# Latent attention: q and k without their rotated part made channels-first, rotated parts turned four heads at a time, scores of two heads side by side

## The chip, the cores and the metric

One core of a Trainium2 chip runs the whole program; the other cores are idle. The metric is the device time of one execution in microseconds, the median of three runs. The program is one fp32 forward pass through two models behind one another, and all matrix weights are streamed from HBM once.

## The reference

`x` is 256 tokens x 1024 channels. A first block has a state-space layer and an attention layer; a second block has two layers (`DEPTH2`), each with three branches (latent attention, convolution, retention) that are gated and merged, and a feed-forward part. The change touches only the latent attention of these two layers:

```python
q = (rms_norm_2(c_q, q_norm) @ w_uq).reshape(B, S, 8, 64 + 32)      # c_q: 256 channels
q_nope, q_pe = q[..., :64], apply_rope(q[..., 64:], cos, sin)
kv = (rms_norm_2(c_kv, kv_norm) @ w_ukv).reshape(B, S, 8, 64 + 64)  # c_kv: 128 channels
k_nope, v = kv[..., :64], kv[..., 64:]
k_pe = apply_rope(k_pe, cos, sin)                                   # one, shared by all heads
s = einsum('bqhd,bkhd->bhqk', q_nope, k_nope) + einsum('bqhr,bkr->bhqk', q_pe, k_pe)
p = softmax(s * 96 ** -0.5)                                         # no mask: 256 x 256
o = einsum('bhqk,bkhd->bqhd', p, v)
```

## The kernel before

**Weights.** A list of slots (up to two k-tiles of 128 x 512 weights each) is streamed by SP into six or eight buffers. Each slot is split: ScalarE copies it to fp32r as `weights_hi` (`make_hi`, L1249), VectorE takes the rest, `weights_lo` (`make_lo`, L1780), and TensorE makes each product from three fp32r matmuls, hi x hi, hi x lo and lo x hi. `tile_slot` (L705 to L707) has 128 tokens as the stationary operand and streams the weights (512 columns wide, 384 for `uq`), so its result has tokens on the partitions; `hidden_slot` (L683 to L685) has 128 weight columns as the stationary operand and streams 256 tokens, so its result has channels on the partitions. `run(n)` does the next n slots of the list. ScalarE and VectorE walk the same list in program order, up to `AHEAD` = 4 slots ahead of TensorE, and empty the accumulators (`evac`) where a chunk of slots ends. The four accumulator banks `acc` are used by parity of the chunk: chunk n waits for the reader of chunk n - 2 (`reader_of`).

**Latent attention of a layer.** `lat_norm_T` is turned (L800) and split into `mla_F_hi` and `mla_F_lo`. Two slots `uq` (two k-tiles, 384 columns: four heads of 96) and two slots `ukv` (one k-tile, 512 columns) make `mla_q_T`, `mla_k_T` and `mla_v_T` with tokens on the partitions. VectorE rotates 32 of each head's 96 channels (`mla_rope`) and writes the shared rotated k into all eight heads. Then `heads` goes over eight heads, one at a time: TensorE turns q and k of the head (four transposes to 96 x 128, L1004), ScalarE copies them to `m_qk_F` (L1612), TensorE makes the scores with a contraction over 96 rows (two matmuls of 256 columns, L1020), VectorE finds the maximum, ScalarE takes the exponential and divides (L1630, L1606), TensorE turns the probabilities (four transposes, L1013), ScalarE copies them, and for every second head `mla_product` multiplies two heads at once: each has 64 value channels, and the two write to partitions 0 to 63 and 64 to 127 of one bank, two column halves of the array (L1071).

**What fills the time between these steps.** Each step is followed by `mla_gap`, which runs two slots of ordinary weight work (retention and gate projections, 36 slots of a layer), so that the other engines have time. The order on each engine is written out by hand; waits are on semaphores. VectorE also has the 31 taps of the convolution (`taps`) spread over the gaps.

A plain fp32 matmul leaves two MATMUL records in the trace, a transpose or an fp32r matmul one.

## Time and profile before

| | |
|---|---|
| median of three runs | 1236.92 us (1236.46 to 1237.2) |
| the profiled execution | 1240.36 us |
| its span | 1238.5 us |
| TensorE busy | 1207.6 us, 98% |
| VectorE busy | 902.3 us, 73% |
| ScalarE busy | 638.7 us, 52% |
| granted TensorE clock | 0.998 of 2.4 GHz |

The span is what the profiler saw between the first and last instruction; the profiled execution took 1.9 us more than that and 3.4 us more than the median of the runs. In the timeline a row is a run of like instructions: start, time, engine, line, operation, tiles and count. TensorE is pipelined, so a record's length (0.39 us for 512 columns) is not what it costs; the distance of the starts is.

### The profile page before, as it was taken

Reading aid. Unit: us, or ns where it says so; the run is one execution under the profiler, and the core shown is the slowest. Engines: PE = TensorE matmul, PEld = TensorE weight load, DVE = VectorE, ACT = ScalarE, POOL = GpSimd, SP = SyncE. Lnnn points to the kernel's source line nnn. Section 1 sums busy time; section 2 is a strip of 40 time slices with the busy share of each in tenths; the row PEclk is TensorE's granted clock in tenths of the full one; section 3 lists DMA queues with packets and bytes.
Section 4 is the critical chain, followed back from the end, with each engine's and each line's share of the span. In section 5 each row is a group of like instructions: output and inputs, shape, how many; then the busy total and the mean of one; then the engine's idle time right before and its main releaser. Section 6 shows DMA issues by size and latency. Waiting matters only on the chain.

```text
span 1238.5 us, 19034 instructions
## 1 busy us (share of the span) xinstructions
PE 1207.6 (98%) x7597; PEld 1015.8 (82%) x7597; DVE 902.3 (73%) x1463; ACT 638.7 (52%) x1034; POOL 102.3 (8%) x163
## 2 busy tenths in 40 slices
PE   7999999999999999999999999999999999999998
PEld 3566778887978888787999987988788787999986
DVE  7998867767598998687656555589998687665553
ACT  4334565575547665546434443556575535444441
POOL 6400011101000200201000001000200201000000
PEclk9999999999999999999999999999999999999999
DMA  7735566444565455355666664565445355556552
GB/s 253 210 103 178 200 210 191 152 130 154 162 202 166 151 160 188 124 179 170 208 187 187 187 190 155 174 217 171 154 153 180 139 174 170 188 195 196 191 194 75
DMA packets 71958, 215.68 MB, mean 174 GB/s; under 512 B 16256, under 2 KB 19744, under 8 KB 71744
## 3 DMA queue, kind: packets, MB, share of 16 engines
q1 hardware_dynamic: 65008, 206.37, 52.0%
q0 software_dynamic: 2112, 6.97, 1.9%
q10 hardware_dynamic: 4752, 1.14, 0.4%
q8 instruction: 60, 0.98, 0.3%
q14 instruction: 26, 0.21, 0.1%
HBM read 208.95 MB, written 3.15 MB: 171 GB/s over the span
## 4 chain that ended last, share of the span: by engine, by line
PE 82%; DVE 10%; ACT 5%; issue 2%; POOL 1%; DMA 0%; SPq 0%; DVEq 0%; POOLq 0%; ACTq 0%
PE acc L705 16%; PE acc L706 16%; PE acc L707 16%; PE acc L683 7%; PE acc L684 7%; PE acc L685 7%; PE acc L642 3%; DVE weights_lo L1780 2%; PE mixed L1020 1%; ACT junk L1284 1%; PE mixed L1117 1%; PE turned L760 1%; ACT weights_hi L1249 1%; DVE h_T L1810 1%; PE mixed L1004 1%
## 5 line engine op out<-in xcount | busy, mean ns | idle before, releaser
L1780 DVE TENSOR_TENSOR weights_lo<-weights_raw,weights_hi 128x1024 fp32r<-128x1024 f32 (+1 forms) x304 | 356.1, 1206 | 67.2 <-ACT weights_hi L1249 66.3
L1249 ACT ACTIVATE weights_hi<-weights_raw 128x1024 fp32r<-128x1024 f32 (+1 forms) x304 | 305.6, 1043 | 77.2 <-DMA weights_raw<-stream_dram 77.0
L705 PE MATMUL acc<-weights_hi,act_F_hi 128*128 128x512 f32 (+1 forms) x656 | 264.8, 404 | 4.2 <-DVE weights_lo L1780 2.5
L707 PE MATMUL acc<-weights_hi,act_F_lo 128*128 128x512 f32 (+1 forms) x656 | 256.7, 391 | 0.0
L706 PE MATMUL acc<-weights_lo,act_F_hi 128*128 128x512 f32 (+1 forms) x656 | 256.5, 391 | 0.0
L683 PE MATMUL acc<-act_F_hi,weights_hi 128*128 128x256 f32 x624 | 175.1, 281 | 0.0
L684 PE MATMUL acc<-act_F_hi,weights_lo 128*128 128x256 f32 x624 | 173.9, 279 | 0.0
L685 PE MATMUL acc<-act_F_lo,weights_hi 128*128 128x256 f32 x624 | 173.9, 279 | 0.0
L705 PEld LDWEIGHTS acc<-weights_hi,act_F_hi 128*128 128x128 f32 x656 | 123.6, 188 | 32.6 <-DVE weights_lo L1780 3.6
L707 PEld LDWEIGHTS acc<-weights_hi,act_F_lo 128*128 128x128 f32 x656 | 123.4, 188 | 26.8
L706 PEld LDWEIGHTS acc<-weights_lo,act_F_hi 128*128 128x128 f32 x656 | 123.7, 189 | 24.0
L685 PEld LDWEIGHTS acc<-act_F_lo,weights_hi 128*128 128x128 f32 x624 | 118.3, 190 | 0.0
L683 PEld LDWEIGHTS acc<-act_F_hi,weights_hi 128*128 128x128 f32 x624 | 117.3, 188 | 0.2
L684 PEld LDWEIGHTS acc<-act_F_hi,weights_lo 128*128 128x128 f32 x624 | 117.3, 188 | 0.2
L1810 DVE SCALAR_TENSOR_TENSOR conv_acc_F<-conv_in_F,conv_params,conv_acc_F 128x256 f32<-128x256 f32 x240 | 98.0, 480 | 0.0
L1780 DVE TENSOR_TENSOR weights_lo_more<-weights_raw_more,weights_hi_more 128x1024 fp32r<-128x1024 f32 (+1 forms) x60 | 71.5, 1215 | 18.0 <-ACT weights_hi_more L1249 17.8
L1810 DVE SCALAR_TENSOR_TENSOR ffn_tanh_F<-ffn_tanh_F,acc 128x512 f32<-128x512 f32 (+1 forms) x24 | 15.4, 642 | 93.4 <-ACT ffn_tanh_F L1369 88.8
L1249 ACT ACTIVATE weights_hi_more<-weights_raw_more 128x1024 fp32r<-128x1024 f32 (+1 forms) x60 | 61.6, 1048 | 26.0 <-DMA weights_raw_more<-stream_dram 25.8
L1369 ACT ACTIVATE ffn_tanh_F<-acc 128x512 f32<-128x512 f32 x20 | 12.0, 598 | 119.1 <-PE acc L685 119.1
L642 PE MATMUL acc<-weights_raw,hn_F 128*128 128x512 f32 x128 | 59.1, 609 | 1.2 <-DMA weights_raw<-stream_dram 1.2
L683 PE MATMUL acc<-act_F_hi,weights_hi_more 128*128 128x256 f32 x208 | 58.2, 280 | 0.0
L684 PE MATMUL acc<-act_F_hi,weights_lo_more 128*128 128x256 f32 x208 | 57.9, 279 | 0.0
(351 smaller groups left out, 1969.6 us busy)
## 6 DMA issues: line engine op xcount, KB each, us to landing
weights_raw<-stream_dram SPq DMA_DIRECT2D x306, 512.0 KB, 3.6
weights_raw_more<-stream_dram SPq DMA_DIRECT2D x58, 512.0 KB, 3.6
gains<-rows_dram POOLq DMA_DIRECT2D x12, 512.0 KB, 4.7
weights_raw<-stream_dram SPq DMA_DIRECT2D x6, 416.0 KB, 3.1
weights_raw<-stream_dram SPq DMA_DIRECT2D x4, 384.0 KB, 3.9
x_T<-x_in_dram SPq DMA_DIRECT2D x4, 256.0 KB, 6.4
ssm_bc<-ssm_bc_dram SPq DMA_DIRECT2D x1, 1024.0 KB, 8.1
u_scratch<-u_T ACTq DMA_DIRECT2D x4, 256.0 KB, 6.2
```

Of the source, the lines that this page charges most:

```text
L642: i = pe.matmul(acc[par][t][:, 0:w], f0[:, k, t * P:(t + 1) * P], whole(pos, slice(kk * w, (kk + 1) * w)), start=first and kk == 0, stop=l ...
L683: pe.matmul(o, wh, hi[:, k, :], start=first and kk == 0 and m % 2 == 0, stop=False, skip_group_check=True)
L684: pe.matmul(o, wl, hi[:, k, :], start=False, stop=False, skip_group_check=True)
L685: i = pe.matmul(o, wh, lo[:, k, :], start=False, stop=last and kk == s["nk"] - 1, skip_group_check=True)
L705: pe.matmul(o, xh, wh, start=first and kk == 0, stop=False)
L706: pe.matmul(o, xh, wl, start=False, stop=False)
L707: i = pe.matmul(o, xl, wh, start=False, stop=last and kk == s["nk"] - 1)
L760: i = pe.transpose(turned_bank[n % 2][:, kk * P:(kk + 1) * P], src(t, 4 * half + kk), ident)
L1004: x = pe.transpose(b[0:dk, (2 * n + t) * P:(2 * n + t + 1) * P], src(t, i), ident)
L1249: act.activation(high(s, slice(0, n)), whole(s, slice(0, n)), ACT.Copy).then_inc(hi_made, 1)
L1780: dve.tensor_tensor(low(s, slice(0, n)), whole(s, slice(0, n)), high(s, slice(0, n)).bitcast(F32), ALU.subtract).then_inc(lo_made, 1)
L1810: return dve.scalar_tensor_tensor(out=o, in0=a, scalar=s, in1=b, op0=op0, op1=op1)
```

## The change

Four things change in both layers. (1) The 64 unrotated channels of q and k of two heads are made with channels on the partitions (`latent_slot`, `qn` and `kn`: head 2p on partitions 0 to 63, head 2p + 1 on 64 to 127); the rotated parts of q of all eight heads come with the second `uq` slot, with tokens on the partitions; v as before. The split of a `uq` slot goes to two tiles in three pieces. (2) The rotated q is turned for four heads at once and the rotated k once, written four times over (`turned_rope`: six transposes a layer instead of 32). (3) The scores of two heads are made together: first contraction over 64 rows, head 2p in rows 0 to 63 of the array and head 2p + 1 in rows 64 to 127, into two banks; then the rotated part, contraction over 32 rows, added into the same banks (`mla_scores`). (4) The order goes by pairs: probabilities of two heads are turned together, and into the banks `turned`. `mla_gap` stands 18 times with work in it, as before.

```diff
-                mq = sb("mla_q_T", [P, TT, MLA_H, MQK], F32, s5)
-                mk = sb("mla_k_T", [P, TT, MLA_H, MQK], F32, s5)
-                mv = sb("mla_v_T", [P, TT, MLA_H, MV], F32, s5)
...
+                sb("latent_lows", [P, 1024], F32, s5)
+                qn = sb("mla_q_nope_F", [P, MLA_H // 2, SEQ], F32, s5)
+                mq = sb("mla_q_rope_T", [P, TT, MLA_H, ROPE], F32, s5)
+                mk = sb("mla_k_rope_T", [P, TT, 4, ROPE], F32, s5)
+                qr = sb("mla_q_rope_F", [P, 2, SEQ], F32, s5)
+                kr = sb("mla_k_rope_F", [P, SEQ], F32, s5)
+                kn = sb("mla_k_nope_F", [P, MLA_H // 2, SEQ], F32, s5)
+                mv = sb("mla_v_T", [P, TT, MLA_H, MV], F32, s5)
...
-                "uq.": (mla_q_copied, 4 * l + n), "ukv.": (mla_v_copied, 4 * l + n),
+                "uq.": (mla_copied, 7 * l + (n - 1 if i else 1)), "ukv.": (mla_copied, 7 * l + 3 + n),
...
+            def latent_slot(s, par):
+                _, kind, half = split_name(s["chunk"])
+                q = kind == "uq."
+                k0 = 0 if q else QR // P
+                pe.wait_ge(lo_made, pos + 1 - WHOLE)
+                for t in range(TT):
+                    who, value = reader_of(acc_user[par], t)
+                    pe.wait_ge(who, value)
+                for kk in range(s["nk"]):
+                    for m in range(2):
+                        cols = slice(m * P, (m + 1) * P)
+                        wh = high(pos, slice(kk * SEQ + m * P, kk * SEQ + (m + 1) * P))
+                        wl = uq_lo[:, half, kk, cols] if q else ukv_lo[:, half, cols]
+                        o = acc[par][0][:, m * SEQ:(m + 1) * SEQ]
+                        pe.matmul(o, wh, c_hi[:, k0 + kk, :], start=kk == 0 and m == 0, stop=False, skip_group_check=True)
+                        pe.matmul(o, wl, c_hi[:, k0 + kk, :], start=False, stop=False, skip_group_check=True)
+                        i = pe.matmul(o, wh, c_lo[:, k0 + kk, :], start=False, stop=kk == s["nk"] - 1, skip_group_check=True)
+                if q and not half:
+                    return i
+                for t in range(TT):
+                    for kk in range(s["nk"]):
+                        xh, xl = (f[:, k0 + kk, t * P:(t + 1) * P] for f in (c_hi, c_lo))
+                        if q:
+                            wh, wl = uqr_hi[:, kk, :], uqr_lo[:, kk, :]
+                        else:
+                            wh, wl = high(pos, slice(4 * NOPE, 4 * (NOPE + MV))), ukv_lo[:, half, 4 * NOPE:]
+                        o = acc[par][1][:, t * SEQ:(t + 1) * SEQ]
+                        pe.matmul(o, xh, wh, start=t == 0 and kk == 0, stop=False, skip_group_check=True)
+                        pe.matmul(o, xh, wl, start=False, stop=False, skip_group_check=True)
+                        i = pe.matmul(o, xl, wh, start=False, stop=kk == s["nk"] - 1, skip_group_check=True)
...
+                def turned_rope():
+                    pe.wait_ge(mla_roped, 2 * TT * (l + 1))
+                    b = mix(f"L{l}.mla.qr", qk_copied, HEADS + 2 * l + 1)
+                    for n in range(2):
+                        for t in range(TT):
+                            x = pe.transpose(b[:, n * SEQ + t * P:n * SEQ + (t + 1) * P],
+                                             mq[:, t, 4 * n:4 * n + 4, :].rearrange("p h d -> p (h d)"), ident)
+                    x.then_inc(mixed, 1)
+                    b = mix(f"L{l}.mla.kr", qk_copied, HEADS + 2 * l + 2)
+                    for t in range(TT):
+                        x = pe.transpose(b[:, t * P:(t + 1) * P], mk[:, t, :, :].rearrange("p h d -> p (h d)"), ident)
+                    x.then_inc(mixed, 1)
+                def mla_scores(pair):
+                    pe.wait_ge(mla_copied, 7 * l + 6)
+                    pe.wait_ge(qk_copied, HEADS + 2 * (l + 1))
+                    heads_of = [2 * pair + e for e in range(2)]
+                    b = [mix(f"L{l}.mla.s{h}", probs_made, 2 * (HEADS + MLA_H * l + h + 1)) for h in heads_of]
+                    for qt in range(TT):
+                        for e in range(2):
+                            rows_ = slice(NOPE * e, NOPE * (e + 1))
+                            pe.matmul(b[e][:, qt * SEQ:(qt + 1) * SEQ], qn[rows_, pair, qt * P:(qt + 1) * P], kn[rows_, pair, :],
+                                      start=(qt == 0), stop=False, skip_group_check=True)
+                    for qt in range(TT):
+                        for e in range(2):
+                            a = NOPE * e + ROPE * (pair % 2)
+                            x = pe.matmul(b[e][:, qt * SEQ:(qt + 1) * SEQ], qr[a:a + ROPE, pair // 2, qt * P:(qt + 1) * P],
+                                          kr[a:a + ROPE, :], start=False, stop=(qt == TT - 1), skip_group_check=True)
+                            if qt == TT - 1:
+                                x.then_inc(mixed, 1)
+                def turned_probs(pair):
+                    pe.wait_ge(probs_scaled, 2 * (HEADS + MLA_H * l + 2 * pair + 2))
+                    wait_turned(len(turn_at))
+                    for e in range(2):
+                        probs_at[f"L{l}.{2 * pair + e}"] = pos
+                        for qt in range(TT):
+                            for kt in range(TT):
+                                n = 2 * kt + qt
+                                x = pe.transpose(turned_bank[e][:, n * P:(n + 1) * P], m_p[:, e, qt, kt * P:(kt + 1) * P], ident)
+                        x.then_inc(mla_probs_turned, 1)
...
-                heads(f"L{l}.mla", MLA_H, MQK, lambda t, h: mq[:, t, h, :], lambda t, h: mk[:, t, h, :], m_qk, m_p, m_pt,
-                      HEADS + MLA_H * l, False, lambda h: (mla_roped, 2 * TT * (l + 1)), mla_gap, mla_product,
-                      [lambda: turned_ret_qk(0), lambda: turned_ret_qk(1)])
+                turned_rope()
+                mla_gap()
+                for i in range(MLA_H // 2 + 1):
+                    if i > 0:
+                        turned_probs(i - 1)
+                    if i < MLA_H // 2:
+                        mla_scores(i)
+                    else:
+                        turned_ret_qk(0)
+                    mla_gap()
+                    mla_gap()
+                    if i == MLA_H // 2:
+                        turned_ret_qk(1)
+                    if i > 0:
+                        mla_product(i - 1)
+                    mla_gap()
+                    mla_gap()
                 for h in range(2, RH):
...
-                act.activation(high(s, slice(0, n)), whole(s, slice(0, n)), ACT.Copy).then_inc(hi_made, 1)
+                if ".uq." in slots[s]["chunk"]:
+                    for o, x in uq_high(s):
+                        i = act.activation(o, x, ACT.Copy)
+                    i.then_inc(hi_made, 1)
+                elif ".ukv." in slots[s]["chunk"]:
+                    act.activation(by_part(high(s, slice(0, n))), by_head(whole(s, slice(0, n))), ACT.Copy).then_inc(hi_made, 1)
+                else:
...
                         act.activation(conv_t[:, t, :], b, ACT.Tanh, scale=0.5).then_inc(read, 1)
-                    elif kind == "uq.":
-                        act.activation(mq[:, t, 4 * i:4 * i + 4, :], b.rearrange("p (h d) -> p h d", h=4), ACT.Copy).then_inc(read, 1)
+                    elif kind in ("uq.", "ukv.") and t == 0:
+                        act.activation((qn if kind == "uq." else kn)[:, 2 * i:2 * i + 2, :].rearrange("p h q -> p (h q)"),
+                                       acc[table[name]["par"]][0][:, :], ACT.Copy).then_inc(read, 1)
+                    elif kind == "uq." and i == 1:
+                        act.activation(mq[:, :, :, :].rearrange("p t h d -> p (t h d)"), acc[table[name]["par"]][1][:, :],
+                                       ACT.Copy).then_inc(read, 1)
                     elif kind == "ukv.":
-                        v = b.rearrange("p (h d) -> p h d", h=4)
-                        act.activation(mk[:, t, 4 * i:4 * i + 4, 0:NOPE], v[:, :, 0:NOPE], ACT.Copy)
-                        act.activation(mv[:, t, 4 * i:4 * i + 4, :], v[:, :, NOPE:NOPE + MV], ACT.Copy).then_inc(read, 1)
+                        act.activation(mv[:, :, 4 * i:4 * i + 4, :],
+                                       acc[table[name]["par"]][1][:, :].rearrange("p (t h d) -> p t h d", t=TT, h=4),
+                                       ACT.Copy).then_inc(read, 1)
                     elif kind == "ret." and i < 4:
                         act.activation(rv[:, t, odd], b, ACT.Copy).then_inc(read, 1)
                     elif kind == "ret.":
```

TensorE in the first of the two layers, one step of the heads before. Names: `mla_q_T` and `mla_k_T` are q and k with tokens on the partitions, `m_qk_F` both turned; rows with 512 columns are slots, three a k-tile and tile of tokens.

```order
L1071 MATMUL turned<-m_probs_T,mla_v_T 64x256 x4
L1004 MATMUL mixed<-consts,mla_q_T 96x128 x2
L1004 MATMUL mixed<-consts,mla_k_T 96x128 x2
L705 MATMUL acc<-weights_hi,act_F_hi 128x512
...
L1013 MATMUL mixed<-consts,m_probs 128x128 x4
L1020 MATMUL mixed<-m_qk_F 128x256 x2
L705 MATMUL acc<-weights_hi,act_F_hi 128x512
```

The same place with the change, a step of a pair of heads:

```order
L1176 MATMUL turned<-consts,m_probs 128x128 x8
L1157 MATMUL mixed<-mla_k_nope_F,mla_q_nope_F 128x256 x4
L1162 MATMUL mixed<-mla_k_rope_F,mla_q_rope_F 128x256 x4
L772 MATMUL acc<-weights_hi,act_F_hi 128x512
...
L1188 MATMUL turned<-m_probs_T,mla_v_T 64x256 x4
L772 MATMUL acc<-weights_hi,act_F_hi 128x512
```

The four transposes ahead of every head are gone; the two score matmuls of a head are now eight of a pair, half over 64 and half over 32 rows; the product stands between slots instead of ahead of transposes. Ahead of the first pair the new transposes stand once:

```order
L1139 MATMUL mixed<-consts,mla_q_rope_T 128x128 x4
L1144 MATMUL mixed<-consts,mla_k_rope_T 128x128 x2
```

ScalarE where the four latent slots are emptied, before (names: `conv_tanh` is the reader of the chunk ahead of them):

```order
L1343 ACTIVATE conv_tanh<-acc 128x512 x2
L1249 ACTIVATE weights_hi<-weights_raw 128x1024
L1345 ACTIVATE mla_q_T<-acc 128x384 x2
L1249 ACTIVATE weights_hi<-weights_raw 128x1024
L1345 ACTIVATE mla_q_T<-acc 128x384 x2
L1348 ACTIVATE mla_k_T<-acc 128x4x64
L1349 ACTIVATE mla_v_T<-acc 128x256
```

and with the change:

```order
L1479 ACTIVATE conv_tanh<-acc 128x512 x2
L1385 ACTIVATE weights_hi<-weights_raw 128x1024
L1481 ACTIVATE mla_q_nope_F<-acc 128x512
L1385 ACTIVATE weights_hi<-weights_raw 128x1024
L1481 ACTIVATE mla_q_nope_F<-acc 128x512
L1484 ACTIVATE mla_q_rope_T<-acc 128x512
L1481 ACTIVATE mla_k_nope_F<-acc 128x512
L1487 ACTIVATE mla_v_T<-acc 128x2x256
```

Twelve copies of a layer are now seven wider ones, at the same place among the splits of the weights.

## Rows read from the trace of the kernel before

**Rows 1.** The page: busy time by engine, and the chain by engine.

```profile
PE 1207.6 (98%) x7597; PEld 1015.8 (82%) x7597; DVE 902.3 (73%) x1463; ACT 638.7 (52%) x1034; POOL 102.3 (8%) x163
PE 82%; DVE 10%; ACT 5%; issue 2%; POOL 1%; DMA 0%; SPq 0%; DVEq 0%; POOLq 0%; ACTq 0%
```

**Rows 2.** Busy time by window: the heads of both layers (length, then engines).

```profile
361.80:482.00 120.20, 120.20 (x579) 97.27 (x578) 111.86 (x213) 74.23 (x141) 6.70 (x1) 1.00 0.52 163
833.00:953.00 120.00, 120.00 (x576) 97.07 (x575) 111.52 (x213) 74.81 (x143) 6.69 (x1) 1.00 0.50 163
```

**Rows 3.** Timeline of TensorE: transposes of the first head among slots.

```profile
361.76 0.39 PE L707 MATMUL acc<-weights_hi,act_F_lo 128*128 128x512 f32 x1
361.99 0.38 PE L1004 MATMUL mixed<-consts,mla_q_T 128*96 128x128 f32 x2
...
362.66 0.40 PE L706 MATMUL acc<-weights_lo,act_F_hi 128*128 128x512 f32 x1
```

**Rows 4.** Timeline of TensorE: scores of the first head among slots.

```profile
367.70 0.40 PE L707 MATMUL acc<-weights_hi,act_F_lo 128*128 128x512 f32 x1
367.94 1.03 PE L1020 MATMUL mixed<-m_qk_F 96*128 96x256 f32 x4
...
369.03 0.39 PE L706 MATMUL acc<-weights_lo,act_F_hi 128*128 128x512 f32 x1
```

**Rows 5.** Timeline of TensorE: product of two heads, columns split in halves.

```profile
399.68 0.40 PE L707 MATMUL acc<-weights_hi,act_F_lo 128*128 128x512 f32 x1
400.00 1.08 PE L1071 MATMUL turned<-m_probs_T,mla_v_T 128*64 128x256 f32 x8
401.02 0.42 PE L1004 MATMUL mixed<-consts,mla_q_T 128*96 128x128 f32 x2
...
401.73 0.40 PE L706 MATMUL acc<-weights_lo,act_F_hi 128*128 128x512 f32 x1
```

**Rows 6.** Timeline of TensorE: eight tiles of 64 rows x 32 columns, two row halves.

```profile
99.07 2.03 PE L913 MATMUL turned<-c_mats_alt,states 64*32 64x128 f32 x128
101.03 2.41 PE L642 MATMUL acc<-weights_raw,hn_F 128*128 128x512 f32 x5
```

**Rows 7.** Groups of instructions by form: weight loads of 128 and of 64 columns.

```profile
L1020 PEld LDWEIGHTS mixed<-m_qk_F 96*128 96x128 f32 x64 | 11.0, 190 | 1.0
L1071 PEld LDWEIGHTS turned<-m_probs_T,mla_v_T 128*64 128x64 f32 x64 | 3.9, 136 | 3.6 <-issue 2.5
```

**Rows 8.** Timeline of TensorE: the latent slots of the first layer.

```profile
332.37 0.33 PE L705 MATMUL acc<-weights_hi,mla_F_hi 128*128 128x384 f32 x1
...
336.54 0.39 PE L705 MATMUL acc<-weights_hi,mla_F_hi 128*128 128x512 f32 x1
...
339.28 0.39 PE L705 MATMUL acc<-weights_hi,act_F_hi 128*128 128x512 f32 x1
```

**Rows 9.** Timeline of ScalarE at the same place.

```profile
332.58 1.08 ACT L1343 ACTIVATE conv_tanh<-acc 128x512 f32<-128x512 f32 x2 [0.24 <-PE acc L685]
336.19 1.06 ACT L1249 ACTIVATE weights_hi<-weights_raw 128x1024 fp32r<-128x1024 f32 x1 [0.66 <-DMA weights_raw<-stream_dram]
337.15 0.85 ACT L1345 ACTIVATE mla_q_T<-acc 128x384 f32<-128x384 f32 x2
```

**Rows 10.** Timelines of VectorE and TensorE: after the rotation, first layer.

```profile
344.11 5.76 DVE L1780 TENSOR_TENSOR weights_lo<-weights_raw,weights_hi 128x1024 fp32r<-128x1024 f32 x5
344.54 0.40 PE L707 MATMUL acc<-weights_hi,act_F_lo 128*128 128x512 f32 x1
345.38 0.50 PE L705 MATMUL acc<-weights_hi,act_F_hi 128*128 128x512 f32 x1 [0.44 <-DVE weights_lo L1780]
```

**Rows 11.** Timelines of ScalarE and TensorE: the latent slots of the second layer.

```profile
807.82 0.85 ACT L1345 ACTIVATE mla_q_T<-acc 128x384 f32<-128x384 f32 x2
...
802.66 0.28 PE L684 MATMUL acc<-act_F_hi,weights_lo 128*128 128x256 f32 x1
...
803.23 0.33 PE L705 MATMUL acc<-weights_hi,mla_F_hi 128*128 128x384 f32 x1
```

189 lines of the change are left out of this document (138 added, 51 removed).

## The prediction

> **What bounds the kernel now.** I read the page first: TensorE is busy 98% of the span and is 82% of the chain that ended last [rows 1]. Then busy time by window, for the two stretches in which the heads run: TensorE has no gap in either, VectorE is busy 111.9 of 120.2 us and ScalarE 74.2 us [rows 2]. So in these stretches time is what TensorE's own instructions take, and work taken from ScalarE or VectorE (12 copies of a layer become seven, eight copies of `m_qk_F` become two) gives nothing by itself. The change has to pay on TensorE, or in a wait of TensorE. I therefore read TensorE's timeline for the distance of starts. The slots give the rule: 12 matmuls of 512 columns from 336.54 to 339.28 are 0.228 us each, 24 of 384 columns from 332.37 are 0.174 us each [rows 8], and five starts of 256 columns from 802.66 to 803.23 are 0.114 us each [rows 11].
>
> **Transposes, the gain.** From the last slot matmul ahead of a head's four transposes to the second one behind them there are 0.90 us [rows 3]; two slot matmuls are 0.46 us of it, so four transposes cost 0.44 us, 0.11 us each. The change takes out 32 a layer and puts in six: 52 fewer in two layers, **5.7 us** less. Nothing covers them before, and nothing else would have run in that time, since TensorE waits for nobody there.
>
> **Scores, streaming: nothing.** Two score matmuls of a head (four records) cost 369.03 - 367.70 - 0.46 = 0.87 us [rows 4], 0.218 us a record, so a pair of heads 1.74 us. The pair now issues eight matmuls, 16 records, of the same 256 columns: one behind another 3.49 us, two at a time 1.74 us. Does the chip do two at a time? Two heads' product does it with column halves: eight records, which would be 1.74 us in a row, took 1.02 us [rows 5]. With row halves I have one place, 128 records of 128 columns in eight tiles, 64 rows x 32 columns, in 1.96 us [rows 6]. By the row of the scores a record of 128 columns is 0.109 us, so four column tiles alone would need 128 x 0.109 / 4 = 3.5 us: the two row halves ran side by side, and into two banks, as here. I take 1.74 us a pair, no change.
>
> **Scores, changing the shape of the array.** Around the product the trace shows a cost that isn't streaming: from the slot matmul at 399.68 to that at 401.73 are 2.05 us, of which 0.46 are slots, 0.44 the transposes and 0.87 the eight records two at a time; 0.28 us remain, for going to halves and back [rows 5], 0.14 us each way. The product keeps its two. The scores ran on the whole array and had none; now each pair goes from the whole to 64 rows, to 32 rows and back, three changes, 24 in two layers: 24 x 0.14 = **3.4 us** more. From 64 to 32 rows the trace shows nothing. The lower end is nothing at all (from transposes to slots the rows show no such cost [rows 3]); the upper is 0.19 us, since the first weights behind a change are 128 columns here and 64 in the product, and the load record is 190 against 136 ns [rows 7]. I take 0.14 for all 24, because the product is the nearest row. The Trainium skill (TensorEngine Tiling (Array Packing), Key Properties) says that a change of tiling mode drains the engine, and lists 64 and 32 rows as different modes. By it all 24 count; were the step from 64 to 32 rows free, 16 would, 1.1 us less.
>
> **Latent slots.** `uq` is 36 matmuls of 256 columns instead of 24 of 384: 4.10 against 4.17 us; `ukv` 24 of 256 instead of 12 of 512: 2.74 against 2.74 [rows 8, 11]. In two layers **0.1 us** less.
>
> **A wait at the second `ukv` slot.** `latent_slot` waits for both readers of its banks before its first matmul; for the second `ukv` slot these are the two copies behind the second `uq` slot, now 512 columns each, 1.08 us for two such copies [rows 9]. ScalarE comes to them after a split that waited for its DMA until 336.19 and took 1.06 us, so they end at 338.3. TensorE would be there at 332.37 + 48 x 0.114 = 337.8: it waits 0.5 us. Behind it stand all slots, but a cover follows: TensorE stands from 344.77 (344.54 + 0.23) to 345.38 for `weights_lo`, which VectorE makes late because of the rotation [rows 10]. Arriving 0.5 us later it waits 0.1 instead of 0.6, and VectorE, whose k part now writes four heads and not eight, isn't later. First layer: -0.1 us (not counting the cover: +0.5). Second layer: TensorE at 803.23 + 5.47 = 808.7, the copies start at 807.82 + 0.08 at the earliest and end at 809.0: 0.3 us, and no stall follows that would cover it. Together **0.2 us** more; between 0 and 0.8.
>
> **Costed at nothing.** The splits of the two `uq` slots are three pieces on ScalarE and VectorE instead of one; they are made some slots ahead, while VectorE waits. Copies, maxima, exponentials and divisions of the heads are as many as before but come in twos: between a pair's scores and the turning of its probabilities lie eight slots, 22 us, and between turning and product four, 11 us, against some 10 us and 2 us of work. If that cover were gone, each late copy (0.6 us) would be TensorE's. VectorE has 8 us to spare in a stretch of 120 and the same work in it. DMA issues and their order are the same, and SP's waits hang on slots that end within half a us of where they did.
>
> **Sum.** -5.7 + 0 + 3.4 - 0.1 + 0.2 = -2.2 us. It is made on one profiled execution (1240.4 us, span 1238.5), which lies 3.4 us above the median of the runs; no term of it is a share, so I take it off the median: 1236.9 - 2.2 = **1234.7 us**. With a change of shape at 0 it is 1231.3 us; with 0.19 us and the wait at its upper end, 0.8, it is 1236.5: the forecast's own range.
>
> **Rivals.**
>
> *Weight loads are not hidden behind matmuls in row tiles* (slower). Two matmuls at a time have four loads of 128 columns for every two steps; 64 columns more cost 54 ns of load [rows 7], so 128 cost 0.108 us. If the next load for a row half waits until the running matmul of that half is done, each step of 0.218 us becomes 0.326: eight steps a pair, eight pairs, 6.9 us, and 1241.6 us. Against it: slots of 256 columns come every 0.114 us though each has such a load in the same rows, and the eight small tiles kept pace [rows 6], with loads of 32 columns only. It decides as soon as more than a third of each load is exposed. The Trainium skill (TensorE: Matmul & The Clock Gate, The mechanism) says that a load overlaps running matmuls only where the row groups differ. Taken at its word it gives this case; the slots speak against it.
>
> *The halves don't run side by side.* The change then doesn't do what it says: 1.74 us a pair more, 13.9 us, 1248.6 us. Only [rows 6] speaks against it for row halves, and no row has row halves with all 128 columns.
>
> *Waits in twos.* VectorE is 93% busy in the heads [rows 2]. It now does two maxima in a row (each with a wait) before the next splits. If one split of 1.2 us came late once a layer, and the first layer's cover failed, 1.2 x 2 + 0.5 less what the forecast gains: 1237.6 us. TensorE's place four slots behind is against it.
>
> *Changes of shape cost nothing where both sides are ready*: 1231.3 us. The 0.28 us at the product speak against it.
>
> **Chances.** Forecast 0.66, loads exposed 0.10, one behind another 0.04, waits in twos 0.14, free changes 0.06. A difference under 0.2%, 2.5 us, is about what a measurement of this kernel can't tell from none; the forecast sits close to that line, so its 0.66 splits into 0.36 below 1234.4 and 0.30 above. Faster: 0.36 + 0.06 = 0.42. Same: 0.30 + 0.12 = 0.42. Slower: 0.02 + 0.10 + 0.04 = 0.16. The range 1231.3 to 1239.5 leaves out the two slow rivals and a little on either side.
>
> **What would show it.** In the changed profile: 12 transposes of rotated parts and no others for q and k; a pair's eight unrotated records in about 0.9 us and the eight rotated ones in about 0.9 us, with starts two by two; from slot to slot around them 1.74 + 0.4 us. Exposed loads would show as 1.3 us for eight records, no concurrency as 1.74. At the second `ukv` slot a wait of TensorE for ScalarE of 0.3 to 0.5 us, and the stall for `weights_lo` after the first layer's rotation nearly gone. Wrong I would be through any idle time of TensorE inside the heads, or a pair's scores over 2.5 us.

## The result and the profile after

| | us |
|---|---|
| before, median of 4 runs beside the changed kernel | 1237.06 (1236.46 to 1237.70) |
| changed kernel, median of 4 runs | 1261.01 (1260.88 to 1261.99) |
| ratio, 95% interval | 1.0195 [1.0182, 1.0208] |
| profiled execution of the changed kernel: its time, its span | 1260.88, 1259.1 |

The change costs 24 us. The prediction was 1234.7 us with a range to 1239.5, and all but 0.16 of the chance on "faster" and "same": it was wrong. In the lines from here on, a row of waits is: who waited for whom, us in total, times, longest. The page of the changed kernel: busy time, the chain that ended last by engine and by line, and two of the costliest groups.

```profile
PE 1212.1 (96%) x7657; PEld 1012.5 (80%) x7657; DVE 901.5 (72%) x1471; ACT 627.9 (50%) x1020; POOL 96.0 (8%) x163
...
PE 60%; DVE 25%; ACT 9%; issue 3%; POOL 1%; DMA 1%; SPq 0%; DVEq 0%; POOLq 0%; ACTq 0%
PE acc L772 10%; PE acc L774 10%; PE acc L773 10%; DVE weights_lo L1971 8%; PE acc L713 7%; PE acc L714 7%; PE acc L715 7%; DVE conv_acc_F L2001 7%; PE acc L676 3%; ACT weights_hi L1385 2%; PE mixed L1246 1%; ACT m_probs L1845 1%; ACT m_probs L1851 1%; DMA weights_raw<-stream_dram 1%; ACT junk L1420 1%
...
L1971 DVE TENSOR_TENSOR weights_lo<-weights_raw,weights_hi 128x1024 fp32r<-128x1024 f32 x296 | 348.6, 1215 | 98.1 <-ACT weights_hi L1385 97.2
...
L772 PE MATMUL acc<-weights_hi,act_F_hi 128*128 128x512 f32 (+1 forms) x656 | 264.6, 403 | 21.4 <-DVE weights_lo L1971 19.7
```

Against [rows 1] VectorE's busy time is the same within 1 us, but its share of the chain went from 10 to 25% and TensorE's from 82 to 60. Work did not grow; an engine with the same work became the one that others wait for. The last two rows say which wait: over the whole span VectorE's splits (`weights_lo`) stand 97.2 us behind ScalarE's halves (`weights_hi`), 66.3 before, and TensorE's slots 19.7 us behind VectorE's, 2.5 before. The same two head windows as in [rows 2], then TensorE's waits over the whole span, changed and before:

```profile
361.80:482.00 120.20, 111.06 (x520) 85.90 (x519) 96.31 (x184) 63.00 (x125) 4.79 (x1) 0.99 0.47 145
833.00:953.00 120.00, 113.05 (x525) 87.92 (x524) 97.11 (x184) 58.14 (x116) 4.75 (x1) 0.97 0.47 149
```

```profile
PE acc L772 <- DVE weights_lo L1971: 19.7, 14, 3.5
PE acc L705 <- DVE weights_lo L1780: 2.5, 5, 0.7
```

TensorE, gapless before, now idles 9.1 and 7.0 us in the windows, and all three engines do less in the same time. VectorE and ScalarE waiting for each other shows in the waits of 361 to 490 us. The last row is the second one in the kernel before:

```profile
ACT m_probs L1845 <- DVE m_stat L2007: 34.2, 4, 13.0
DVE weights_lo L1971 <- ACT weights_hi L1385: 24.8, 9, 3.2
ACT m_probs L1851 <- DVE m_stat L2722: 16.2, 4, 4.9
DVE weights_lo L1780 <- ACT weights_hi L1249: 7.5, 7, 1.8
```

The first pair of heads, step by step: VectorE's timeline, then ScalarE's (start, length).

```profile
373.62 0.17 DVE L2007 TENSOR_SCALAR m_stat<-m_stat 128x2 f32<-128x2 f32 x1
376.98 2.36 DVE L1971 TENSOR_TENSOR weights_lo<-weights_raw,weights_hi 128x1024 fp32r<-128x1024 f32 x2 [3.19 <-ACT weights_hi L1385]
379.26 3.25 DVE L2001 SCALAR_TENSOR_TENSOR conv_acc_F<-conv_in_F,conv_params,conv_acc_F 128x256 f32<-128x256 f32 x8
382.43 0.22 DVE L2722 RECIPROCAL m_stat<-m_stat 128x2 f32<-128x2 f32 x2
385.30 2.36 DVE L1971 TENSOR_TENSOR weights_lo<-weights_raw,weights_hi 128x1024 fp32r<-128x1024 f32 x2 [2.66 <-ACT weights_hi L1385]
```

```profile
373.09 0.47 ACT L1845 ACTIVATE m_probs<-mixed,m_stat 128x256 f32<-128x256 f32 x1 [6.61 <-DVE m_stat L2007]
...
375.89 2.00 ACT L1385 ACTIVATE weights_hi<-weights_raw 128x1024 fp32r<-128x1024 f32 x2
377.79 1.08 ACT L1491 ACTIVATE h_T<-acc 128x512 f32<-128x512 f32 x2
382.61 1.71 ACT L1851 ACTIVATE m_probs<-m_probs,m_stat 128x256 f32<-128x256 f32 x4 [3.75 <-DVE m_stat L2722]
```

VectorE ends the pair's two maxima at 373.8 and goes straight to its splits. Their halves come only behind ScalarE's four exponentials and four decays, from 375.89: VectorE stands 3.19 us. It then makes eight taps (3.25 us) before the reciprocals, and ScalarE stands 3.75 us for those, with its next halves queued behind the divisions; so VectorE stands another 2.66 us. That is 5.85 us in each of four steps, 23.4 us a layer, on an engine that I had credited with 8 to spare.

Where the 24 us lie: from the transposes of `h` ahead of the heads to those of `conv_acc_F` behind them the first layer takes 202.6 us instead of 191.6, the second 203.1 instead of 190.6: 23.4 us more. TensorE's own instructions take 1.3 us less than before (measured below, on a kernel with the same TensorE instructions and without these waits), so 24.7 us have to be found. Of these TensorE is idle 9.1 and 8.5 us (128.20 - 119.06 and 129.40 - 120.89, windows from 370 and 848 us to the stretch's end), in ten waits. From start to start such a wait costs some 0.25 us more than its idle time (the record ahead of it lasts 0.39 us where the next one would have started after 0.23): 2.5 us. The rest is the clock. After the longest wait, 3.5 us, and after two in the second layer the granted clock falls:

```profile
440.00:448.00 8.00, 6.80 (x23) 5.44 (x24) 5.59 (x12) 4.25 (x8) 0.00 (x0) 0.79 0.12 31
894.00:902.00 8.00, 7.09 (x24) 5.69 (x25) 8.00 (x14) 5.55 (x8) 0.00 (x0) 0.79 0.34 116
918.00:926.00 8.00, 5.64 (x18) 4.57 (x19) 5.66 (x12) 4.25 (x9) 0.00 (x0) 0.79 0.20 66
```

0.79 of 8 us is 3.4 us at the lower level, 1.2 GHz. Compared start by start with the kernel that has the same TensorE instructions and no such waits, the three stretches put TensorE 4.5 us behind; the heads of before have none. 17.6, 2.5 and 4.5 us are 24.6.

TensorE's steps themselves went nearly as forecast, the scores of the first pair:

```profile
367.50 0.40 PE L774 MATMUL acc<-weights_hi,act_F_lo 128*128 128x512 f32 x1
367.83 1.13 PE L1157 MATMUL mixed<-mla_k_nope_F,mla_q_nope_F 64*128 64x256 f32 x8
368.90 1.13 PE L1162 MATMUL mixed<-mla_k_rope_F,mla_q_rope_F 32*128 32x256 f32 x8
369.96 0.51 PE L772 MATMUL acc<-weights_hi,act_F_hi 128*128 128x512 f32 x1
370.30 0.40 PE L773 MATMUL acc<-weights_lo,act_F_hi 128*128 128x512 f32 x1
```

Measured as the prediction measured them, from the last slot matmul ahead to the second behind less two slots, the sixteen records take 370.30 - 367.50 - 0.46 = 2.34 us, where the forecast had 2.16 and two heads before took 1.74. The halves do run side by side and their loads are hidden; three changes of shape cost 0.60 us instead of 0.42. Of that 0.10 us lie ahead of the first record, 0.11 in the slot matmul behind, which takes 0.34 us instead of 0.23, and 0.20 in each of the two phases of eight records, 1.07 us instead of 0.87.

### The profile page after: what moved, and what is told of

The parts are those of the page before. It is cut to its first block, busy times and chain, and to the rows that moved or that the text cites. A ratio compares the mean times of both kernels' runs of the same rounds, so it can differ in the third digit from the quotient of the medians.

```text
span 1259.1 us, 19130 instructions
## 1 busy us (share of the span) xinstructions
PE 1212.1 (96%) x7657; PEld 1012.5 (80%) x7657; DVE 901.5 (72%) x1471; ACT 627.9 (50%) x1020; POOL 96.0 (8%) x163
## 4 chain that ended last, share of the span: by engine, by line
PE 60%; DVE 25%; ACT 9%; issue 3%; POOL 1%; DMA 1%; SPq 0%; DVEq 0%; POOLq 0%; ACTq 0%
PE acc L772 10%; PE acc L774 10%; PE acc L773 10%; DVE weights_lo L1971 8%; PE acc L713 7%; PE acc L714 7%; PE acc L715 7%; DVE conv_acc_F L2001 7%; PE acc L676 3%; ACT weights_hi L1385 2%; PE mixed L1246 1%; ACT m_probs L1845 1%; ACT m_probs L1851 1%; DMA weights_raw<-stream_dram 1%; ACT junk L1420 1%
## 5 line engine op out<-in xcount | busy, mean ns | idle before, releaser
L1971 DVE TENSOR_TENSOR weights_lo<-weights_raw,weights_hi 128x1024 fp32r<-128x1024 f32 x296 | 348.6, 1215 | 98.1 <-ACT weights_hi L1385 97.2
L1385 ACT ACTIVATE weights_hi<-weights_raw 128x1024 fp32r<-128x1024 f32 x296 | 298.3, 1050 | 71.9 <-DMA weights_raw<-stream_dram 71.7
L772 PE MATMUL acc<-weights_hi,act_F_hi 128*128 128x512 f32 (+1 forms) x656 | 264.6, 403 | 21.4 <-DVE weights_lo L1971 19.7
L774 PE MATMUL acc<-weights_hi,act_F_lo 128*128 128x512 f32 (+1 forms) x656 | 259.3, 395 | 0.0
L774 PEld LDWEIGHTS acc<-weights_hi,act_F_lo 128*128 128x128 f32 x656 | 124.6, 190 | 26.6
L2001 DVE SCALAR_TENSOR_TENSOR conv_acc_F<-conv_in_F,conv_params,conv_acc_F 128x256 f32<-128x256 f32 x240 | 106.5, 512 | 0.0
L715 PE MATMUL acc<-act_F_lo,weights_hi_more 128*128 128x256 f32 x208 | 57.5, 276 | 0.0
```

The source lines that it names most:

```text
L715: i = pe.matmul(o, wh, lo[:, k, :], start=False, stop=last and kk == s["nk"] - 1, skip_group_check=True)
L772: pe.matmul(o, xh, wh, start=first and kk == 0, stop=False)
L774: i = pe.matmul(o, xl, wh, start=False, stop=last and kk == s["nk"] - 1)
L1385: act.activation(high(s, slice(0, n)), whole(s, slice(0, n)), ACT.Copy).then_inc(hi_made, 1)
L1971: dve.tensor_tensor(low(s, slice(0, n)), whole(s, slice(0, n)), high(s, slice(0, n)).bitcast(F32), ALU.subtract).then_inc(lo_made, 1)
L2001: return dve.scalar_tensor_tensor(out=o, in0=a, scalar=s, in1=b, op0=op0, op1=op1)
```

## The experiments

Theory A: the order of work on VectorE and ScalarE makes them wait for each other, and VectorE has no room for it. Rival B: TensorE's own new work. Rival C: the granted clock by itself. Rival D: that heads come in pairs, whatever the order. Times are medians, ratios to the kernel before in the same call.

**The order undone, one engine at a time.** Four kernels from the changed one. On VectorE, the taps first:

```diff
+                    n = tapped[0]
+                    tapped[0] = min(n + 1, 2 * MLA_H + 2)
+                    taps(...)
                     run(min(2, fillers[0]))
                     splits(pos + AHEAD)
...
-                    n = tapped[0]
-                    tapped[0] = min(n + 1, 2 * MLA_H + 2)
-                    taps(...)
```

> Edit: in each gap VectorE does its share of the convolution's taps first and its share of the splits behind them, so the halves that ScalarE makes after the exponentials are looked at 3 us later. Theory A (VectorE and ScalarE wait for each other within a step of two heads; 24.8 us of VectorE's idle time in the first layer's heads stand in front of weights_lo): the wait of VectorE for weights_hi behind two maxima shrinks from 3.2 us to under 1, TensorE's waits for weights_lo go, 1236 to 1243 us. Rival B (the 24 us are TensorE's own: row tiles, changes of shape, loads that aren't hidden): 1260 to 1262 us, no change. Rival C (the lower granted clock is a cause of its own): time stays within 5 us of 1261 while the stalls shrink.

1239.04 us (1234.54 to 1240.42, 10 runs), ratio 1.0001 [0.9986, 1.0015]. Moving three lines takes back all of the loss. The waits of 361 to 490 us:

```profile
DVE weights_lo L1971 <- ACT weights_hi L1385: 5.1, 4, 1.7
```

On ScalarE, the divisions late:

```diff
                     mla_gap()
+                    mla_gap()
                     if i < MLA_H // 2:
                         for e in range(2):
                             mla_divide(2 * i + e)
-                    mla_gap()
...
```

> Edit: ScalarE's divisions of a pair stand behind the second gap instead of between the two, so it makes the next halves before it waits for VectorE's reciprocals. Theory A: the second of VectorE's two waits in a step (2.7 us) goes and the first stays (3.2 us); 1246 to 1253 us. Rival B: 1260 to 1262 us.

1243.62 us (1242.87 to 1244.75), ratio 1.0052 [1.0037, 1.0067]: it takes back more than the 1246 to 1253 us that I expected. VectorE's wait for halves fell to 14.1 us, and four waits of 3.2 us are left, as said.

Both edits together:

> Edit: the taps first and the divisions late, both. Theory A: both of VectorE's waits for weights_hi go; 1233 to 1239 us, as I forecast for the change as it stands. Rival B: 1260 to 1262 us. Between (1245 to 1255 us) would say that a wait remains that neither order removes, the burst of two maxima itself.

1237.06 us (1234.70 to 1240.66, 10 runs), ratio 0.9998 [0.9985, 1.0011]. Rival B is out, since TensorE does exactly the changed kernel's work here, and C with it: without the waits the granted clock in both layers' heads is 1.00 again.

ScalarE's decays ahead of the steps (`for h in range(RH): decays(h)` behind `copied_rope()`, and none in a step):

> Edit: ScalarE's four decays are made before the heads' steps and not one pair in each step between the exponentials and the gap. Theory A: the stretch in which ScalarE makes no halves gets about 1 us shorter in each of 8 steps; 1252 to 1256 us. Rival B: 1260 to 1262 us.

1264.94 us (1263.24 to 1266.81), ratio 1.0219 [1.0202, 1.0236]: a miss. The wait behind the maxima fell by 1 us in each step, as expected (3.19 to 2.21), but the four decays now stand ahead of the first halves, where VectorE waits 4.28 us. VectorE's waits of 361 to 490 us are the same 25 us in other places:

```profile
DVE weights_lo L1972 <- ACT weights_hi L1385: 25.6, 11, 4.3
```

I had counted what left the steps and not where it went.

**Is it the pairs, or the order?** Heads one at a time again on VectorE and ScalarE, the order inside a gap (splits, then taps) kept. VectorE's part; ScalarE's exponentials and divisions are moved alike:

```diff
-                        for e in range(2):
-                            mla_max(2 * i + e)
+                        mla_max(2 * i)
                     mla_gap()
...
-                        for e in range(2):
-                            mla_inverse(2 * i + e)
+                        mla_max(2 * i + 1)
+                        mla_inverse(2 * i)
                     mla_gap()
+                    if i < MLA_H // 2:
+                        mla_inverse(2 * i + 1)
```

> Edit, in the changed kernel: VectorE's maxima and reciprocals, ScalarE's exponentials and divisions of a pair's two heads stand one gap apart again instead of together; TensorE's work and the order inside a gap (splits, then taps) stay. Theory A: VectorE's wait behind the first maximum falls from 3.2 to about 2 us, and a second one of 1 to 2 us comes behind the other maximum, but the wait at the divisions goes; 1243 to 1255 us. Theory D (the twos alone): 1235 to 1240 us. Rival B (TensorE's own work): 1260 to 1262 us.

1280.97 us (1277.28 to 1287.56), ratio 1.0356 [1.0317, 1.0395]: outside every range, and the worst of all. Three gaps of a step now begin with a split behind something that ScalarE can't have finished:

```profile
376.96 2.36 DVE L1972 TENSOR_TENSOR weights_lo<-weights_raw,weights_hi 128x1024 fp32r<-128x1024 f32 x2 [3.07 <-ACT weights_hi L1385]
386.18 2.36 DVE L1972 TENSOR_TENSOR weights_lo<-weights_raw,weights_hi 128x1024 fp32r<-128x1024 f32 x2 [2.82 <-ACT weights_hi L1385]
393.72 2.36 DVE L1972 TENSOR_TENSOR weights_lo<-weights_raw,weights_hi 128x1024 fp32r<-128x1024 f32 x2 [1.93 <-ACT weights_hi L1385]
```

So the twos are not the cause: without them, in this order, the loss is larger, and with them, in the other order (taps first), it is gone. Rival D is out. The counterpart, in the kernel before, first missed its aim: `splits(pos + AHEAD)` ahead of each head's first taps.

> Edit, in the kernel before (one head at a time, no pairs): VectorE makes its splits between a head's maximum and the taps, where before it made taps there and splits only behind the reciprocals. Theory A (what costs is a split of VectorE right behind a maximum, whose halves ScalarE makes only behind the exponentials): VectorE waits for weights_hi behind each maximum, two exponentials and a half, some 1 to 2.3 us in each of 16 heads with 8 us of room a layer; 1240 to 1252 us, though nothing is in pairs. Rival D (only the pairs make the wait long enough): within 2 us of the kernel before, 1235 to 1239 us.

1238.05 us (1236.00 to 1243.53, 10 runs), ratio 1.0007 [0.9988, 1.0026]. This run says nothing: the splits up to that point are mostly made already, ahead of the maximum where a chunk ends, and the edit moved instructions only at the end of the heads. The one split that does lie between two heads' steps is `splits(pos + AHEAD + 1)`, behind the reciprocal. That one moved:

```diff
                     if half:
-                        splits(pos + AHEAD + 1)
                         taps(mid, b)
                     else:
+                        splits(pos + AHEAD + 1)
                         taps(a, mid)
```

> Edit, in the kernel before: the one split that VectorE makes between a head's reciprocal and its second taps stands between the maximum and the first taps instead. TensorE's work and the heads one at a time stay. In this kernel VectorE waits 0.4 to 1.4 us there now, with 4 or 8 taps (1.7 or 3.3 us) between maximum and split. Theory A (room on VectorE against idle time in front of its splits): each wait grows by the taps' time up to the chain of two exponentials, decays and a half, some 2.3 to 3.1 us, 16 times: some 10 us more idle time a layer with about 11 there to spare in all; 1240 to 1256 us without any pair. Rival D (only work in pairs does it): 1236 to 1240 us.

1256.49 us (1255.35 to 1258.82), ratio 1.0157 [1.0141, 1.0173]. One split a head, 1.2 us of work, moved ahead of 4 or 8 of its tap instructions, costs the kernel before 19 us. Its waits of 361 to 490 us (7.5 us in the kernel before), and TensorE's longest over the whole span:

```profile
DVE weights_lo L1780 <- ACT weights_hi L1249: 22.3, 9, 3.1
PE mixed L1013 <- ACT m_probs L1606: 12.3, 4, 5.6
```

VectorE's waits are of the same kind, but they reach TensorE by another way than in the changed kernel: TensorE waits 12.3 us for probabilities, and for `weights_lo` no more than before (2.5 us). VectorE's maxima and reciprocals come late, and ScalarE's exponentials and divisions with them.

**Does the idle time or the room decide?** The changed kernel with 12 of the 31 taps left out, in its own order:

> Edit, in the changed kernel: 12 of the convolution's 31 taps are left out, 48 of VectorE's instructions of 0.41 us a layer, 19.6 us; the order stays. Theory A says that the 24 us of waiting hurt because VectorE had only 8 us to spare in these 120: with some 28 to spare its waits stay about as they are (each of 2.7 to 3.2 us) and TensorE's waits for weights_lo nearly go; 1234 to 1242 us. If each of the waits reached TensorE by itself, however much room VectorE has: 1255 us or more. Rival B: 1260 to 1262 us.

1237.21 us (1235.65 to 1241.71, 10 runs), ratio 0.9992 [0.9973, 1.0012]. The waits are as long and more of them (first row, 361 to 490 us), and TensorE's are no longer than in the kernel with both edits, 2.0 us (second row, the whole span):

```profile
DVE weights_lo L1971 <- ACT weights_hi L1385: 28.5, 12, 3.2
```

```profile
PE acc L772 <- DVE weights_lo L1971: 2.0, 4, 0.7
```

Side by side, the first layer's windows from 370 us to the first transposes behind the heads; idle is length less busy:

| kernel | length | VectorE busy | VectorE idle | TensorE idle |
|---|---|---|---|---|
| before | 117.4 | 106.3 | 11.1 | 0 |
| taps first | 116.9 | 106.8 | 10.1 | 0 |
| both edits | 116.8 | 107.9 | 8.9 | 0 |
| divisions late | 118.4 | 105.4 | 13.0 | 1.4 |
| before, one split moved | 127.0 | 106.0 | 21.0 | 6.5 |
| changed | 128.2 | 104.6 | 23.6 | 9.1 |
| decays first | 130.9 | 106.9 | 24.0 | 8.6 |
| one at a time | 137.9 | 106.8 | 31.1 | 14.2 |
| changed, fewer taps | 117.8 | 89.1 | 28.7 | 0 |

TensorE needs 117 us, VectorE some 106: the room is 11 us. VectorE's work is nearly the same in all rows but the last, so that its idle time grows with the length by construction; what the table shows is where TensorE starts to be idle. With up to 11 us of VectorE's idle time it isn't, with 13.0 it is 1.4 us, and with 21 to 31 us 6.5 to 14.2. That VectorE's waits come first and don't merely follow from a longer stretch is shown by the edits, which move VectorE's or ScalarE's instructions alone, and by the last row: with 89 us of work 28.7 us idle are free.

**TensorE's terms.** First, on the kernel with both edits, a pair's matmuls in the order head, then tile of tokens (`for e` outside `for qt`):

> Edit, on the changed kernel with the taps first and the divisions late: a pair's score matmuls in the order head, then tile of tokens, so that the two matmuls of one row half follow each other. If the two row halves of the array run side by side in the change's order, half of that is lost: from 2.22 us a pair (last slot matmul to next, less 0.23) to between 2.6 and 3.9 us, 3 to 14 us in all, 1240 to 1251 us. If they never ran side by side: 2.2 us a pair and 1237 us as before the edit.

1240.31 us (1235.63 to 1245.56, 10 runs), ratio 1.0012 [0.9989, 1.0036], and 2.46 us from slot to slot, as with the order of the change:

```profile
368.99 0.40 PE L774 MATMUL acc<-weights_hi,act_F_lo 128*128 128x512 f32 x1
369.31 1.14 PE L1157 MATMUL mixed<-mla_k_nope_F,mla_q_nope_F 64*128 64x256 f32 x8
370.38 1.14 PE L1162 MATMUL mixed<-mla_k_rope_F,mla_q_rope_F 32*128 32x256 f32 x8
371.45 0.50 PE L772 MATMUL acc<-weights_hi,act_F_hi 128*128 128x512 f32 x1
```

Eight records of 0.218 us in a row would be 1.74 us a phase; 1.07 is two at a time (0.87) and a change of shape. It doesn't need the matmuls of the two halves to alternate in the program.

Then the price of a change of shape: the rotated part on 64 rows too, so that 8 of the 24 changes go. k is kept in two copies, the other head's 32 rows multiplied by zero.

```diff
+        rope_mask = sb("rope_mask", [P, 2], F32)
...
-                    act.activation(kr[:, :], b[:, 0:SEQ], ACT.Copy)...
+                    act.activation(kr[:, :], b[:, 0:SEQ], ACT.Copy, scale=rope_mask[:, 0:1])
+                    act.activation(mk[...], b[:, 0:SEQ], ACT.Copy, scale=rope_mask[:, 1:2])...
...
-                            x = pe.matmul(b[e][...], qr[a:a + ROPE, ...], kr[a:a + ROPE, :], ...)
+                            x = pe.matmul(b[e][...], qr[rows_, ...], k_[rows_, :], ...)
```

> The kernel with the taps first and the divisions late once more, beside the next one on the same chip: 1235 to 1241 us, in two groups some 4 us apart, by whether a long run of matmuls of 256 columns comes every 0.113 or every 0.118 us.

> Edit, on the same kernel: the rotated part of the scores runs in row halves of 64 as the unrotated one, against two copies of k in which the other head's 32 rows are zero (one copy more on ScalarE a layer, products with zeros); the step from 64 to 32 rows in each pair is gone, 8 changes of shape of 24. Theory: a change costs some 0.2 us of TensorE, and the phase streams as long as before; a pair's scores take 2.0 instead of 2.22 us from slot to slot, 1.6 us in all, 0.1% of the whole, which the medians can hardly show and the trace must. If the step from 64 to 32 rows is free, as I held possible: no difference in the trace. If streaming follows the rows (64 against 32): the phase gets longer and the gain is gone.

The base again: 1236.31 us (1234.80 to 1240.45, 12 runs), ratio 0.9998 [0.9987, 1.0009]. The edit: 1251.41 us (1250.69 to 1252.12), ratio 1.0115 [1.0099, 1.0130]. The trace shows the 0.2 us a pair gained, but the whole is 15 us longer: slot matmuls come every 0.2325 us instead of 0.229, also where the edit does nothing. The new tile of 8 bytes a partition had moved every later tile; that this is enough is shown by the run with tiles moved alone, below.

> Edit, against the run with both parts of the scores on 64 rows: the tile that holds the row masks has 16 columns instead of two, 64 bytes a partition instead of 8, nothing else. Theory E (the 8 bytes moved every later tile in SBUF, and matmuls of 512 columns came every 0.2325 us instead of 0.2289; some 3300 of them, 12 us): they come every 0.229 us again, and the whole is the kernel with the taps first and the divisions late less the 1.6 us of the saved changes of shape, 1233 to 1239 us. Rival F (the masked copies or the products with zeros made TensorE slower everywhere, or that run's chip was slow): 1249 to 1253 us as before.

1244.73 us (1243.29 to 1246.06), ratio 1.0062 [1.0048, 1.0075]: neither. 64 bytes further, matmuls of 512 columns are a little faster than in the base (0.2276 us, mean over the first layer's heads, against 0.2292), those of 256 columns slower (0.1193 us in the feed-forward blocks). So, with no tile moved (the mask in `rows_offset`, 64 bytes that nothing used), and, apart from it, with the tiles moved by 8 bytes and no instruction changed (`rows_offset` of 18 columns instead of 16):

> Edit, against the run with both parts of the scores on 64 rows: the row masks lie in a spacer of 64 bytes a partition that the kernel already has, so no tile moves. Theory (8 changes of shape at some 0.2 us): slot to slot around a pair's scores 2.25 us instead of 2.45, each of the two layers' head stretches 0.8 us shorter than in the kernel with the taps first and the divisions late (190.7 and 190.2 us from the layer's first transposes of h to the heads' end), matmuls of 512 columns every 0.229 us; 1233 to 1238.5 us in all. Rival F (masked copies, products with zeros): 1243 us or more.

> Edit, in the kernel with the taps first and the divisions late: the spacer of 64 bytes is 72 bytes long, so all tiles behind it lie 8 bytes further; no instruction changes. Theory E (addresses set the pace of TensorE's matmuls): 512 columns every 0.2325 us instead of 0.229, 1248 to 1254 us. Rival F: no change, 1235 to 1241 us.

Moved only: 1252.94 us (1252.54 to 1253.90), ratio 1.0118 [1.0095, 1.0141]. From one `L774` to the third behind it, nine slot matmuls, 0.233 us each:

```profile
365.21 0.39 PE L774 MATMUL acc<-weights_hi,act_F_lo 128*128 128x512 f32 x1
...
367.31 0.39 PE L774 MATMUL acc<-weights_hi,act_F_lo 128*128 128x512 f32 x1
```

Unmoved: **1234.46 us** (1232.63 to 1238.24, 12 runs), ratio **0.9972 [0.9956, 0.9988]**, the only version faster than both kernels. The masks and the products with zeros cost nothing that the time shows.

```profile
368.17 0.40 PE L774 MATMUL acc<-weights_hi,act_F_lo 128*128 128x512 f32 x1
368.50 1.13 PE L1157 MATMUL mixed<-mla_k_nope_F,mla_q_nope_F 64*128 64x256 f32 x8
369.46 1.03 PE L1163 MATMUL mixed<-mla_k_rope_F,mla_q_rope_F 64*128 64x256 f32 x8
370.42 0.50 PE L772 MATMUL acc<-weights_hi,act_F_hi 128*128 128x512 f32 x1
370.76 0.39 PE L773 MATMUL acc<-weights_lo,act_F_hi 128*128 128x512 f32 x1
```

2.25 us from slot to slot instead of 2.46: a change of shape costs **0.2 us**. The head stretches shrank by less than the 0.8 us expected, to 190.4 and 189.5 us from 190.8 and 190.2.

## Why the prediction was wrong

**The step that failed** is "Costed at nothing", in its sentence on work in twos: "between a pair's scores and the turning of its probabilities lie eight slots, 22 us ... against some 10 us and 2 us of work", "VectorE has 8 us to spare in a stretch of 120 and the same work in it". The first half is true of the probabilities: TensorE never waits for them. But VectorE and ScalarE also feed every slot, and I compared their work with the time, not their order with each other. The changed kernel has `splits` ahead of `taps` in VectorE's `mla_gap`, right behind the maxima, where before the taps stood between maximum and reciprocal. A reader of the code can price it from the rows: two maxima, then four exponentials, four decays and a half, is 3.2 us of waiting against 3.3 us of taps that could have stood there. Four such steps and their echo at the divisions are 23 us a layer against 11 of room.

**The rival "waits in twos"** named the engine, and priced it as one late split of 1.2 us a layer, 1237.6 us. It recurs in each step, twice, and is of 3.2 and 2.7 us. What I held against it, TensorE's place four slots behind, didn't hold: in the windows TensorE is idle 9.1 and 8.5 us.

**Transposes:** right. Measured as the 0.44 us of four before, six cost 0.66 us a layer (361.34 to 362.46 us less two slots), 0.11 each, so the 5.7 us are saved.

**Scores, streaming: nothing:** right, and now shown in row halves with 128 columns. **Exposed loads** and **halves not side by side** both fall with it.

**Changes of shape:** mis-sized. I took 0.14 us with an upper bound of 0.19; it is 0.20, three in 0.60 us a pair and one in what the run with 64 rows in both parts saves. 24 changes are 4.8 us, not 3.4. The 0.28 us for two that I took it from stood in a row in which transposes follow the product. Between slots, where the changed kernel has it, the product costs more:

```profile
406.17 0.40 PE L774 MATMUL acc<-weights_hi,act_F_lo 128*128 128x512 f32 x1
406.50 1.08 PE L1188 MATMUL turned<-m_probs_T,mla_v_T 128*64 128x256 f32 x8
...
407.85 0.40 PE L773 MATMUL acc<-weights_lo,act_F_hi 128*128 128x512 f32 x1
```

407.85 - 406.17 - 0.46 = 1.22 us, so 0.35 for two changes. Six products have that new place: 0.4 us more that the sum had nowhere. The Trainium skill (TensorEngine Tiling (Array Packing), Key Properties and Available Configurations) has a change of mode drain TensorE, and 64 and 32 rows as two modes. The run that takes that step away agrees, 0.2 us each.

**Latent slots:** 0.1 us less was forecast, more was measured. The 36 matmuls of `uq` take 336.56 - 332.23 = 4.33 us, 0.120 each, not 0.114 (4.17 us before), and the 24 of `ukv` 2.9 us instead of 2.74:

```profile
332.23 0.28 PE L737 MATMUL acc<-mla_F_hi,weights_hi 128*128 128x256 f32 x1
...
336.56 0.28 PE L737 MATMUL acc<-mla_F_hi,weights_hi 128*128 128x256 f32 x1
...
337.86 0.28 PE L752 MATMUL acc<-weights_hi,mla_F_lo 128*128 128x256 f32 x1
338.07 0.36 PE L737 MATMUL acc<-mla_F_hi,weights_hi 128*128 128x256 f32 x1
```

The last row is the second `ukv` slot: it starts 0.21 us behind the matmul ahead of it, so 0.09 us late and not 0.5. In the kernel with both edits it is 0.34 us late, in the second layer under 0.1 in both, where 0.3 was forecast. The 0.44 us stall at 345.38 of [rows 10] is gone, as forecast.

**The sum on TensorE alone:** forecast -2.2 us. The kernel with both edits takes 190.76 and 190.23 us for the two head stretches against 191.63 and 190.64: -1.3 us. Most of even that is luck. The slot matmuls in the heads, some 430 a layer, come every 0.2292 us on average instead of 0.2304, 1.0 us in two layers, which is no term of my sum; the terms that are leave 0.3 us. The changed kernel's tiles lie at other places than those of before, and the runs above show that this can set the pace; whether it does so here stays open. That kernel's median is 0.5 us below that of before, and the interval holds no change. Had VectorE's order been kept, the time would have lain in the forecast's range, with the gain itself not shown; as it is, a gain of 1 us was bought with a loss of 25.

## What to carry to other kernels

When two engines feed a third, busy shares say how much room there is and the order says how much of it is idle: write out, for each pair of engines that wait for each other in both directions, what stands between what one hands over and what it next needs back, and put there the work that depends on nobody. When steps are regrouped, check each helper's inner order again. And before judging a change by its time, see whether it moved tiles in memory: an edit that costs 1% may be an address.

## What the runs showed of the hardware

**The place of tiles in SBUF sets TensorE's pace.** All tiles behind one spacer 8 bytes further and no instruction changed: 0.233 instead of 0.229 us for a matmul of 512 columns, 0.117 instead of 0.113 for one of 256 (means over the first layer's feed-forward block), some 15 us in all, ratio 1.0118 against 0.9998 for the same instructions in place. Why the place matters, and which tile's does, no run shows.

**Matmuls of 256 columns come at one of two paces, and stay with it.** 30 us of the second layer's feed-forward block in the kernel with the taps first, then in that with both edits, at the same granted clock:

```profile
1100.00:1130.00 30.00, 30.00 (x258) 30.00 (x257) 15.63 (x19) 12.93 (x17) 0.00 (x0) 1.00 0.59 192
```

```profile
1100.00:1130.00 30.00, 30.00 (x267) 30.00 (x267) 17.96 (x20) 14.74 (x18) 0.00 (x0) 1.00 0.57 194
```

0.118 against 0.113 us, 4 us over the block. It differs between executions of one kernel: that with both edits was profiled twice, and has 0.113 us there once and 0.118 the other time. It would explain the two groups of times of these kernels, near 1235.5 and near 1239.5 us; also why the profiled execution of before lay 3.4 us above the median: from its transposes of `ffn_hid_F` to the next layer's of `h` the first layer's block took 163.6 us, those of the changed kernel and of both edits 159.8. Only profiled executions show the pace, and what picks it stays open.

**Two row halves overlap in whatever order their matmuls are issued,** at least within eight records.

**A stall can cost more than its length.** Behind TensorE's wait of 3.5 us, which ended at 441.2 us, the granted clock was 1.2 instead of 2.4 GHz for 3.4 us from 442.4 us on, up to 1.7 us lost. It isn't so behind each: after a wait of 2.4 us that ended at 894.9 us the clock fell at 896.4, after one of 2.4 us that ended at 415.7 it stayed, and in the kernel with the divisions late it stayed at 1.00 through both layers' heads, with waits of up to 2.4 us.
